# One core, two transformer blocks: modulation block 9 summed on VectorE and loaded last, and the gate of token tile 1 placed behind the first expert search

## The reference, cut to what matters

```python
mod_lat = (silu(c) @ w_ada[l] + b_ada[l])[:, None, :]
sh1, sc1, gt1, sh2, sc2, gt2 = split(mod_lat, 6, axis=-1)
...
mla_lat, mla_ctx = mla_mixer(...)
ml_lat, ml_ctx = mlstm_mixer(...)     # ends with sigmoid(o) * rmsnorm(h, g_out)
x = x + gt1 * (concatenate([mla_lat, ml_lat], -1) @ w_out[l])
h2 = rmsnorm(x, g_norm2[l]) * (1.0 + sc2) + sh2
x = x + gt2 * peer(h2, w_pq[l], sub_keys[l], expert_u[l], expert_v[l])
```

```python
g = softmax(best, axis=-1)
act = gelu(einsum('thkd,td->thk', expert_u[eidx], xb), approximate=False)
return einsum('thk,thkd->td', (g * act), expert_v[eidx])
```

## Time and profile before

| | us |
|---|---|
| median of 3 runs | 1897.13 |
| lowest, highest | 1894.73, 1901.65 |
| the profiled execution's own time | 1897.57 |
| its span in the trace | 1895.8 |

### The profile page before, as it was taken

One profiled execution on the slowest core, in us unless ns is written; L12 is line 12 of the kernel. 1 busy time (PEld: TensorE's weight loads), 2 busy tenths in 40 slices (PEclk: granted clock), 3 DMA queues, 4 the chain that ended last, 5 costly groups with the idle time before them and its releaser, 6 DMA issues.

```text
span 1895.8 us, 19298 instructions
## 1 busy us (share of the span) xinstructions
PE 1689.9 (89%) x6418; PEld 1013.9 (53%) x6418; DVE 883.4 (47%) x2176; ACT 553.1 (29%) x1507; POOL 580.6 (31%) x601
## 2 busy tenths in 40 slices
PE   6999898889898777777779988999999998899998
PEld 2545464444453222222236766777764767587775
DVE  1476667776665757564432444311223345332112
ACT  2233333443434343343312432211111252221111
POOL 0000026777777777777600022100000003110000
PEclk9999999999999999999989999999999999999999
DMA  9647129999999999999965210654442321084510
GB/s 338 251 165 255 62 95 406 409 409 409 409 408 409 406 392 409 409 405 406 408 221 178 89 45 1 228 164 151 134 167 72 137 89 38 3 275 147 166 65 23
DMA packets 173305, 438.56 MB, mean 231 GB/s; under 512 B 12291, under 2 KB 58531, under 8 KB 173076
## 3 DMA queue, kind: packets, MB, share of 16 engines
q0 software_dynamic: 81824, 299.99, 40.5%
q1 hardware_dynamic: 91382, 137.33, 20.9%
HBM read 436.23 MB, written 1.05 MB: 231 GB/s over the span
## 4 chain that ended last, share of the span: by engine, by line
PE 59%; DMA 21%; DVE 6%; POOL 5%; issue 4%; ACT 3%; DVEq 1%; SPq 0%; ACTq 0%; POOLq 0%
DMA arena<-in_expert_u,indices 20%; PE psum L1035 15%; PE psum L1046 6%; PE psum L823 4%; PE psum L757 3%; POOL arena L1153 3%; DVE activations_T L1991 3%; POOL arena L1150 2%; PE psum L620 2%; PE psum L1056 2%; PE psum L1024 2%; PE psum L853 1%; PE psum L1006 1%; PE psum L503 1%; PE psum L928 1%
## 5 line engine op out<-in xcount | busy, mean ns | idle before, releaser
L1991 DVE CUSTOM_DVE_ANT_0 activations_T<-arena,psum 128x1024 f32<-128x1024 f32 x256 | 312.7, 1222 | 242.9 <-DMA arena<-in_expert_u,indices 238.6
L730 PE MATMUL psum<-arena 128*128 128x512 f32 x512 | 284.4, 637 | 122.3 <-ACT arena L1403 121.6
L1035 PE MATMUL psum<-activations_T,weight_ring 128*128 128x256 f32 x1280 | 279.2, 379 | 0.0
L1150 POOL DMA_INDIRECT arena<-in_expert_u,indices x256 | 245.6, 959 | 106.3 <-DVE activations_T L1991 61.7
L1153 POOL DMA_INDIRECT arena<-in_expert_v,indices x256 | 243.5, 951 | 81.0 <-issue 72.6
L731 PE MATMUL psum<-arena 128*128 128x512 f32 x512 | 265.1, 600 | 0.0
L1035 PEld LDWEIGHTS psum<-activations_T,weight_ring 128*128 128x128 f32 x1280 | 243.0, 190 | 39.8 <-issue 7.6
L730 PEld LDWEIGHTS psum<-arena 128*128 128x128 f32 x512 | 81.5, 190 | 304.2 <-ACT arena L1403 278.2
L2216 DVE SCALAR_TENSOR_TENSOR arena<-psum,small,arena 128x254 f32<-128x254 f32 (+1 forms) x176 | 76.8, 478 | 322.2 <-ACT arena L1543 318.6
L1112 POOL TENSOR_TENSOR small<-small 128x1 f32<-128x1 f32 (+4 forms) x29 | 30.3, 1046 | 606.8 <-DVE small L2105 240.4
L731 PEld LDWEIGHTS psum<-arena 128*128 128x128 f32 x512 | 98.2, 192 | 124.2 <-issue 124.2
(11 more groups left out here) (387 smaller groups left out, 2057.7 us busy)
## 6 DMA issues: line engine op xcount, KB each, us to landing
weight_ring<-in_ffn_w_in SPq DMA_DIRECT2D x44, 1024.0 KB, 7.7
weight_ring<-in_w_in SPq DMA_DIRECT2D x15, 2048.0 KB, 12.9
weight_ring<-in_w_ada SPq DMA_DIRECT2D x12, 2048.0 KB, 13.3
arena<-in_ffn_w_out POOLq DMA_DIRECT2D x22, 1024.0 KB, 5.3
weight_ring<-in_w_out SPq DMA_DIRECT2D x6, 2048.0 KB, 7.9
weight_ring<-in_w_pq SPq DMA_DIRECT2D x4, 2048.0 KB, 15.4
weight_ring<-in_w_in SPq DMA_DIRECT2D x2, 2080.0 KB, 8.6
arena<-in_expert_u,indices POOLq DMA_INDIRECT x256, 11.1
```

The costliest lines, as they stand in the source:

```text
L730: mm(o0, DIAG[:, n % ND, :], VROWS[n % NV][:, 0:512], start=m == 0, stop=m == PICKS - 1)
L1035: ins = mm(o[:, wh * SEQ:(wh + 1) * SEQ], w[:, k, wh * 256 + g * P:wh * 256 + (g + 1) * P], XTP[:, k, :], start=k == 0, stop=k == KT - 1)
L1150: nc.gpsimd.indirect_dma_start(UROWS[g % NU], None, a["expert_u"], bass.IndirectOffsetOnAxis(ap=where, axis=0)).then_inc(sem(f"u_row{g % N ...
L1991: ttr(out=DOTJ, in0=UROWS[n % NU], in1=h2, scale=1.0, scalar=0.0, op0=ALU.mult, op1=ALU.add, accum_out=DOT[:, i, m:m + 1]).then_inc(sem("u ...
```

## The change

Block 9 of the modulation is computed as blocks 4 to 8, 10 and 11 are: DVE makes the eight steps and PE one matmul of summation. It is loaded behind blocks 10 and 11. Its accumulator is the one of block 11, `MACL`, so its steps begin when block 11 has been summed. The steps are run two at a time: behind the addition of block 11 in batch n = 1; in batch n = 2 ahead of the mean of tile 0's squares, behind the gate of tile 0, and at the end of the batch. PE takes a bank for the sum, `spare`, ahead of the two banks of tile 0's output, and makes the sum behind tile 0's turn. DVE adds the bias at the end of batch n = 2, with a `drain` behind it. PE's wait for ACT's copy of the turn is moved out of `gated` to its two callers; in batch n = 2 it now stands behind the sum.

The mean and the gate of tile 1 stand behind the whole of `search(0)` instead of within it.

```diff
-        ada_loads(8, 12)
+        for b in (8, 10, 11, 9):
+            ada_loads(b, b + 1)
...
-            at["ada"], modulated = {}, iter(range(1, 8))
+            at["ada"], modulated = {}, iter(range(1, 9))
...
-            def modulation_sum(b):
+            def modulation_sum(b, o=None):
                 pe.wait_ge(sem("mod_read"), next(modulated))
-                o = bank_d()
-                mm(o, ONE, (MACL if b >= 10 else MACC)[:, b % 2, :], start=True, stop=True).then_inc(d_full, 1)
+                o = bank_d() if o is None else o
+                mm(o, ONE, (MACL if b >= 9 else MACC)[:, b % 2, :], start=True, stop=True).then_inc(d_full, 1)
...
             mla()
-            modulation(9, 10)
             pe.wait_ge(sem("lf_ready"), 1)
...
             vector_weights(10)
             vector_weights(11)
+            vector_weights(9)
...
                 ins.then_inc(a_full, 1)
-                pe.wait_ge(a_free, at["gated"])
...
                 if n == 2:
                     wout += [weights(512), weights(512)]
+                    spare = bank_d()
                     outputs = [bank_d() for b in range(2)]
                     for b in range(2):
                         output(outputs[b], 0, b, 0, 4)
                     o = bank_a()
                     at["gated"] = c["a"]
                     gated(0, o)
+                    modulation_sum(9, spare)
+                    pe.wait_ge(a_free, at["gated"])
...
             gated(1, o)
+            pe.wait_ge(a_free, at["gated"])
...
             mla_probabilities()
-            modulation(9, 10)
-            late = weighted(11)
+            late = chain(weighted(11), weighted(9))
...
                     if n == 2 and hh == 0:
+                        two_late()
                         mean_of([(0, 4, VD)])
...
                 if n == 2:
                     gate(0)
-                if n < 2:
+                if n < 3:
                     two_late()
                 mla()
...
                 if n < 2:
                     modulation(10 + n, 11 + n)
+                if n in (1, 2):
+                    two_late()
                 if n == 2:
+                    modulation(9, 10)
+                    dve.drain()
                     dve.wait_ge(sem("g2_in"), 16)
...
-            for step in enumerate(search(0)):
-                if step[0] == 8:
-                    mean_of([(4, 8, VD)])
-                if step[0] == 10:
-                    gate(1)
+            all_of(search(0))
+            mean_of([(4, 8, VD)])
+            gate(1)
             pick_softmax(0)
```

More of the change, by code:

```diff
@@ L14 @@
 from contextlib import ExitStack
+from itertools import chain
 import numpy as np
@@ L1596, in weighted @@
                 dve.wait_ge(sem(f"w_in{n % WSLOTS}"), landed[n])
-                w, acc = slot8(n, 512), (MACL if b >= 10 else MACC)[:, b % 2, :]
+                w, acc = slot8(n, 512), (MACL if b >= 9 else MACC)[:, b % 2, :]
                 ts(acc, w[:, 0, :], SILC[:, 0, 0:1], None, ALU.mult)
```

## The result

| | before | changed |
|---|---|---|
| median, us (17 runs each) | 1897.48 | 1903.94 |
| lowest to highest | 1894.44 to 1901.65 | 1901.01 to 1907.41 |
| the profiled execution's own time | 1897.57 | 1906.81 |
| its span | 1895.8 | 1905.0 |

The ratio is 1.0033 with a 95% interval of 1.0027 to 1.0040: the changed kernel is slower by 5 to 8 us, clear of the noise but under the 0.5% (9.5 us) of the forecast's "same". With 17 runs of each kernel much less than that 0.5% can be told apart. The profiled execution of the changed kernel is one of its longer ones, 2.9 us over the median.

A forecast was written before the change was run, and what follows sets the result against it. The expert gather was taken as a transfer stage that only shifts, so the first gather's issue time counts. The terms 1.2 + 1.35 + 2.96 + 0.2 + 0.1 - 0.8 = +5.0 us gave 1902 us, own range 1899 to 1905, 8-in-10 range 1896 to 1908.

The forecast's parts named there:

- The gather only shifts: Expert gather stage from 271.83 us: keeps its length and starts with its first gather; wrong if it changes by over 2 us.
- third rival: Tile 1's later output holds back PE's first picks and stalls the gathers, passing on 5.1 us: 1907 us, 10%.
- The removed matmuls: Block 9's eight matmuls on PE, 7.06 us from 159.52: removal gains 0.0 us, as PE then waits for DVE's scaling.
- first rival: The matmuls taken off PE count for 7.06 us, with the bank hidden and the gate worth 2.1: 1888 us, 7%.
- Pair 1: Two block 9 steps on DVE at the end of batch 1, ahead of the reduction: on the path, +1.2 us.
- Pair 2 and 4: Block 9 steps on DVE ahead of batch 2's mean and behind its combination: hidden by DVE's waits, 0.0 us for the former.
- Pair 3: Block 9 steps on DVE behind tile 0's gating, ahead of the reduction: +1.67 us less 0.32 hidden by ACT, +1.35.
- The bank: Bank taken early: tile 0's output product on PE waits for the first score product's bank, +2.96 us.
- The sum of block 9: One summing matmul of 0.89 us on PE, where PE waits for ACT's copy: +0.2 us.
- The clock: PE's output product starts at the low clock again after a longer pause: +0.1 us.
- rival of a low clock: PE's clock falls at unit 1 or twice at the output product: +1.7 us, 1904 us, 8%.
- The gate: Tile 1's gate behind the search: indices 2.1 us earlier, but POOL's root precedes the first gather, so only -0.8 us.

The follow-up runs named there:

- x2: The changed kernel once more, on a chip with a slower gather: 1997.06 us, with 114.26 us from the forget gates' result to the first gather.
- e2: The changed kernel with the mean and the gate of tile 1 back inside the search: ratio 1.0034 to the kernel before.
- e1: The kernel before with only the mean and the gate of tile 1 moved behind the search: ratio 1.0000 to the kernel before.
- e3: The kernel before with only the gate of tile 1 behind the search, its mean left inside: ratio 1.0001 to the kernel before.
- e4: The changed kernel with the second bank of tile 0's output taken only behind the first one's four matmuls: ratio 1.0024 to the kernel before.
- e6: The changed kernel with DVE scaling unit 0's probabilities ahead of block 10's eight steps: ratio 1.0024 to the kernel before.
- e7: The kernel before with DVE scaling unit 0's probabilities ahead of block 10's steps: PE's turn 7.06 us, second reduction 11.13 us behind the forget gates' result.
- e9: The changed kernel with the second bank taken late, block 9's first and third pairs in DVE's idle time, tile 1's mean inside the search: ratio 1.0000 to the kernel before.
- e5: The changed kernel with block 9's first and third pairs moved to where DVE idles in batch 2: ratio 1.0012 to the kernel before.
- e8: The kernel before with tile 1's gate behind the search, mean inside, and a block 11 pair moved ahead of the second reduction: ratio 0.9984 to the kernel before.
- x1: The kernel before once more, on a chip with a slower gather: 1999.94 us, with 109.86 us from the forget gates' result to the first gather.

## Why the prediction held, point by point

Forecast 1902 us, +5.0 on the kernel before; measured 1903.94, +6.5; the stretch from `LF` to the gather grew by 5.3 us and, in x2, by 4.4.

By the columns the 5.32 us are 0.71 (to r2), 0.49 (r4 to r6), 1.67 (r6 to r7), 2.65 (to the output product), 0.78 (to the score) and -0.98 (to the gather). The waits alone give 1.22 + 0.36 + 1.67 + 2.65 - 0.98 = 4.9, near the forecast's +5.0, but with one term of 0.36 in it that the forecast did not have. The clock adds 0.71 and 0.8 and takes back 1.09. So the mechanism held, and that the sum came out so close is in part luck.

Of the signs named in advance, the output product starts at 227.35 us, released by the score operation, and the root at 276.98. In a trace that reaches `LF` 1.05 us later these are the 226.3 and, within a us, the 276.8 of the forecast. The reduction of unit 1 is at 174.94 and not at about 173: 1.05 of it is the later `LF`, 0.71 the clock.

- **The gather only shifts:** right at 406 GB/s, 676.1 against 675.9 us; on the other two chips the stage varies by more than the test of 2 us. The third rival (the late output of tile 1) is at most small: the stage was 675.9 and 675.6 us with the gate within the search (before, e2) and 676.1 to 676.8 with it behind (changed, e1, e3, e4).
- **The removed matmuls, 0.0:** right, and shown from both sides by e6 and e7. The first rival fell with e9.
- **Pair 1, +1.2:** 1.22 (e5). The trace after doesn't show it in full: r4 to r6 grew by only 0.49. To the 1.22 comes DVE's idle time, 0.36 on the path, which the forecast had at nothing without looking for it. And 1.09 goes (17.39 against 16.30 where the clock is high), because the product took 3.50 us at a low clock before and 2.05 in the changed kernel:

```profile
194.06 3.50 PE L688 MATMUL psum<-arena,activations_T 128*128 128x128 f32 x16 [0.98 <-ACT activations_T L1362]
```

```profile
195.82 2.05 PE L692 MATMUL psum<-arena,activations_T 128*128 128x128 f32 x16 [0.98 <-ACT activations_T L1367]
```

- **Pair 2 and 4, hidden:** right; DVE still waited 1.75 us for ACT's squares behind pair 2, and pair 4 ended at 233.28, ahead of PE's turn at 236.77.
- **Pair 3, +1.67 less ACT's 0.32:** 1.67, and 0.32.
- **The bank, +2.96:** e4 gives back 2.65, which is 2.96 - 0.32 + 0.01: the difference of the two releases by the copy and by the score product, with ACT's cover in it. I had put the cover with pair 3; the sum is the same. Where pair 3 is not there, the bank's price can be read in full: 4.23 in e5 against 1.26, 2.97 us. So the smaller sum that the prediction gave beside its own, by which one more bank costs nothing, is ruled out.
- **The sum of block 9, +0.2:** 0.03 in the rows (from the turn's start to the next product 1.30 us, 1.27 before). I had PE's idle time as 0.67 us, from the end of the turn's row to the product. But PE starts its next matmul 0.44 us behind the turn's start, ahead of that row's end (236.77 and 237.21), so the idle time was 0.83 us, and the sum's 0.86 fit in it.
- **The clock, +0.1:** too small. The output product was 9.59 and 9.42 us long, not 8.80 (+0.8 and +0.6), and unit 1's stretch between 0 and 0.7 longer. I had the rival of a low clock with +1.7. Ahead of the product PE now idles 7.10 us, and the rows show 0.50 from 223 us on, 4 us ahead of the product. "TensorE: Matmul & The Clock Gate", Part 1, of the Trainium skill takes the throttled level as what idling leads back to; the rows agree for these pauses, and the size had to be read from the product, 0.8 us and not another 1.7. They also show that a pause does not settle it: behind the same pause of 2.78 us the product took 8.80 us before and 7.11 in e8, where the clock stayed at 1.00, and at 169 us of the kernel before the clock fell with no pause at all. The forecast read one case of it as the rule.
- **The gate, -0.8:** -0.98. The hop from the root to the gather is 0.18 us where I took 0.28, the distance from the indices to the gather, and the search was 2.17 us shorter, not 2.1.
- **The softmax behind the gate:** covered, as said. DVE's first dot product waits 0.40 us for its row.
- **The remaining 1.1 us** of the 6.5 isn't in the stretch from `LF` to the gather. It may be the second block, which was 950.7 and 954.3 us in the two traces of the changed kernel and 948.0 and 948.2 in those of the kernel before, or the spread of the runs. Over all fourteen traces it was 951.1 us on average with block 9 on DVE (948.2 to 954.3) and 949.6 with it on PE (948.0 to 951.2), a difference smaller than the spread. This stays open.

## What to carry to other kernels

Before work is moved off an engine, look who else arrives at the same wait: here PE and DVE met within 0.1 us, and taking 7 us of matmuls away gained nothing. A buffer taken in a rotation ahead of where it is needed moves every later wait on by one, and the price is to be read as the distance between two releases in the trace, here 2.96 us (2.65 and 2.97 when taken out). A step that is put behind a search or another producer brings what it needs from other engines with it: the root, ahead of the gathers in POOL's program, stood in front of the very gathers that were to start earlier.

## What was not expected of the hardware

Where the granted clock falls ahead of the gather decides as much as the waits: kernels that are equal in a stretch differ there by 1.2 us (r4 to r6 in e1 and e7) or 0.8 us (r2 in the two traces of the changed kernel), and the same output product took 7.11, 8.80, 9.59 and 10.15 us. A gain at one place can be given back at the next, as in e6. The kernel before on a chip where the gather moved 347 instead of 406 GB/s (x1) was 5% slower, all of it in the gather stage (778.0 against 675.9 us). Why the rate differs is not shown; PE's granted clock in that stage was lower there too, 0.88 against 0.99.
